# The first two activation tiles of a two-layer hybrid block, loaded and split one by one around the first weight tile

## Chip, cores, metric

The kernel runs on one core of a Trainium2 chip. The metric is the device time of one execution in microseconds (us). The engines are TensorE (PE, the matrix products), VectorE (DVE), ScalarE (ACT), GpSimd (POOL) and SyncE (SP), which issues the weight loads; data move through 16 DMA engines.

## What is computed

The reference runs two hybrid layers (retention, native sparse attention and a gated linear recurrence, side by side) and then two transformer layers (a dilated window mixer and a block attention mixer, each with a squared-ReLU MLP) on 256 tokens of width 1024. What matters here is its very first step, a matrix product of all tokens with the first input weight:

```python
def hybrid_layer(x, w_in, w_out, ln_g, ln_b, ...):
    proj = x @ w_in                 # x: 256 x 1024, w_in: 1024 x 3352
    ...                             # retention, sparse attention, recurrence
    y = jnp.concatenate([y_ret, y_nsa, y_lru], axis=-1) @ w_out
    return layer_norm(DEEPNORM_ALPHA * x + y, ln_g, ln_b)
```

## The kernel before

**Split products.** Every operand of the big products is held as two rounded parts: a high part, which ScalarE makes by copying the float32 value into a rounded type (`act_hi`, `w_hi`), and a low part, which VectorE makes as the value minus its high part (`act_lo`, `w_lo`). A product is three matmuls: high by high, high by low, low by high.

**Tiles.** The contraction of 1024 is cut into eight tiles k = 0 to 7 of 128 rows. An activation tile is 128 x 256 float32 (128 KB), a weight tile of the first three chunks 128 x 512 (256 KB). A chunk is four weight tiles. The first block of 512 output columns uses chunks 0 and 1. The first `HEAD` = 3 chunks (twelve weight tiles) are loaded, rounded and split tile by tile; all later chunks come whole, in one load of 1 MB (two smaller loads for the block named "window"), and are rounded whole by `split_hi` (L1396) and split whole by `split_lo` (L1881).

**Load order.** SP issues all weight loads from one queue. It begins with `x_pair(0)` (L590), activation tiles 0 and 1 in one load of 256 KB with 2 KB for each of 128 partitions, then weight tiles 0 and 1 (L598), then `x_pair(1)`, weight tiles 2 and 3, and so on. Chunk 3 is issued (L606) once `w_lo_done` says that chunk 0 is split; chunk 6 once chunk 3 is split.

**Rounding and splitting.** ScalarE and VectorE each walk the same list in order: `first_hi(0)` (L1503, both tiles of the pair in one instruction of 128 x 512), `head_hi(0)` (L1829), `head_hi(1)`, `first_hi(1)`, `head_hi(2)`, and so on; VectorE the same with `first_lo` (L2098) and `head_lo` (L2632). The raw activations lie in `y_tok`.

**TensorE at the start.** It waits for a small zeroed tile and multiplies it thirteen times with itself (`warm_up(13)`, L1366; each float32 product shows as two matmuls, 26 in all). Then `first_products` makes the six matmuls of k = 0 for both token halves (L861, L862, L865), the four that need only `w_hi` first. Then come k = 1 to 3, both halves of one k after the other, then k = 4 to 7 of one half after the other (L755 to L757), and `bias_vectors` (L871). ScalarE moves each finished half out of PSUM (L1414) in the middle of its list of rounding steps. GpSimd waits for the fourth `w_hi` before it issues three small constant loads, and for the rounding of chunk 3 before the next ones.

Of the kernel before, what the change touches and what calls it, by code (L numbers as in the profile page):

```python
# [21 lines left out]
S = 256  # L22
# [89 lines left out]
def build(nc, dram, out):  # L112
    F = mybir.dt.float32
    FR = mybir.dt.float32r
    I32 = mybir.dt.int32
    ALU = mybir.AluOpType
    ACT = mybir.ActivationFunctionType
# [47 lines left out]
    HEAD = 3  # L165
# [39 lines left out]
    X0, Y0, X1, Y1, DSW_U, DSW_Y, FFN0_U, MOBA_U, MOBA_Y, FFN1_U = range(10)  # L205
    LRU_CHUNK = [0, 1, 0, 1, 0, 0, 0, 0, 0, 0]
    ACT0 = [sum(ACTS[:i]) // 2 for i in range(11)]
# [29 lines left out]
    with ctx:  # L237
# [3 lines left out]
        def sem(name):  # L241
            return ctx.enter_context(nc.semaphore(name))
# [127 lines left out]
        ident_in = sem("ident_in")  # L370
        x_in = [sem(f"x_in{i}") for i in range(KD // 2)]
        x_rows = sem("x_rows")
        hot_in = sem("hot_in")
        gatew_zero = sem("gatew_zero")
        relb_in = sem("relb_in")
# [10 lines left out]
        at_hi = sem("at_hi")  # L386
# [171 lines left out]
        def first_acts(i):  # L558

            return y.rearrange("p t n -> p (t n)")[:, 512 * i:512 * i + 512]  # L560
# [26 lines left out]
        @block.sync  # L587
        def _(sp):
            def x_pair(i):
                sp.dma_start(first_acts(i), dram["x_features"][:, 2 * i:2 * i + 2, :].rearrange("p k n -> p (k n)")).then_inc(x_in[i], 16)  # L590

            x_pair(0)
            for c, (b, j) in enumerate(CHUNKS):
                d = BLOCKS[b]
                r0 = d["row0"] + 512 * j
                if c < HEAD:
                    for k in range(4):
                        sp.dma_start(w_raw[:, c, k, :], d["w"][r0 + 128 * k:r0 + 128 * k + 128, d["c0"]:d["c0"] + 512]).then_inc(first_in[4 * c + k], 16)  # L598
                        if k % 2 and 4 * c + k < KD - 1:
                            x_pair(2 * c + k // 2 + 1)  # L600
                    continue
                if c >= RAW:
                    sp.wait_ge(w_lo_done, split_count(c - RAW))
                for c0, at, n in pieces(b):
                    src = d["w"][r0:r0 + 512, c0:c0 + n].rearrange("(k p) n -> p k n", p=128)
                    sp.dma_start(w_raw[:, c % RAW, :, at:at + n], src).then_inc(w_arrived[c % RAW], 16)  # L606
            rows = out[0].rearrange("(t p) d -> p t d", p=128)
            for half in range(2):
                sp.wait_ge(acc_free[half], free_count(NB) - 1)
            sp.dma_start(rows[:, :, 0:512], x[:, :, 0:512]).then_inc(out_done, 16)  # L610
            for half in range(2):
                sp.wait_ge(acc_free[half], free_count(NB))
                sp.dma_start(rows[:, half, 512:1024], x[:, half, 512:1024]).then_inc(out_done, 16)
            sp.wait_ge(out_done, 16 * 3)
# [89 lines left out]
        def _(pe):  # L704
# [139 lines left out]
            def first_block():  # L844

                first_products()
                for k in range(1, 4):
                    for half in range(2):
                        tokens(0, half, (k,))
                for half in range(2):  # L850
                    tokens(0, half, range(4, 8))
                bias_vectors()

            def first_products():

                wh, wl = w_hi[:, 0, 0, 0:BLOCKS[0]["n"]], w_lo[:, 0, 0, 0:BLOCKS[0]["n"]]
                pe.wait_ge(at_lo, ACT0[X0] + 1)
                pe.wait_ge(w_hi_done, 1)
                for half in range(2):
                    o = sums(0, half)[:, 0:BLOCKS[0]["n"]]  # L860
                    pe.matmul(o, act_hi[:, 0, 128 * half:128 * half + 128], wh, start=True, stop=False)  # L861
                    pe.matmul(o, act_lo[:, 0, 128 * half:128 * half + 128], wh, start=False, stop=False)  # L862
                pe.wait_ge(w_lo_done, 1)
                for half in range(2):
                    pe.matmul(sums(0, half)[:, 0:BLOCKS[0]["n"]], act_hi[:, 0, 128 * half:128 * half + 128], wl, start=False, stop=False)  # L865
# [497 lines left out]
            def warm_up(count):  # L1363

                for _ in range(count):
                    pe.matmul(ps7[:, 0:128], still, still, start=True, stop=True)  # L1366

            still = st.rearrange("p a n -> p (a n)")
            pe.wait_ge(st_zero, 1)
            warm_up(13)  # L1370
            for l in range(LAYERS):
                hybrid(l)

# [11 lines left out]
        def _(act):  # L1385
# [442 lines left out]
                act.wait_ge(first_in[k], 16)  # L1828
                act.activation(w_hi[:, k // 4, k % 4, :], w_raw[:, k // 4, k % 4, :], ACT.Copy).then_inc(w_hi_done, 1)  # L1829

            for k in range(4 * HEAD):
                if k < KD and k % 2 == 0:
                    first_hi(k // 2)
                head_hi(k)
# [27 lines left out]
        def _(dve):  # L1862
# [766 lines left out]
            def head_lo(k):  # L2629

                dve.wait_ge(w_hi_done, k + 1)
                dve.tensor_tensor(w_lo[:, k // 4, k % 4, :], w_raw[:, k // 4, k % 4, :],  # L2632
                                  w_hi[:, k // 4, k % 4, :].bitcast(F), ALU.subtract).then_inc(w_lo_done, 1)

            for k in range(4 * HEAD):
                if k < KD and k % 2 == 0:
                    first_lo(k // 2)
                head_lo(k)
# [37 lines left out]
```

## Time and profile before

| what | us |
|---|---|
| median of 3 runs | 903.51 |
| lowest and highest of them | 903.37, 903.54 |
| the profiled execution's own time | 903.17 |
| its span, first to last instruction | 901.4 |
| TensorE busy in the span | 893.2 |

The span is what the trace shows; the profiled execution's own time is 1.77 us more, which lies around the span, and it was 0.34 us below the median of the runs. All times in the rows below are counted from the span's start.

### The profile page before, as it was taken

The numbers are of one execution on the slowest core, as the hardware profiler recorded it, in microseconds if no ns is written. First come the engines' busy times: TensorE is split into PE (matmuls) and PEld (weight loads), VectorE is DVE, ScalarE is ACT, GpSimd is POOL, SyncE is SP. The second block draws the span as 40 slices with busy tenths as digits, with TensorE's granted clock in tenths as the row PEclk, the third lists the DMA queues.
The fourth block names the chain that finished last, engine by engine and source line by source line (L and its number), as shares of the span: only waits on it lengthen the run. The fifth ranks groups of instructions, "written<-read, shape, count | busy, mean of one in ns | idle before, by whom it ended". The sixth has DMA issues, their size and how long they took to land.

```text
span 901.4 us, 13857 instructions
## 1 busy us (share of the span) xinstructions
PE 893.2 (99%) x5614; PEld 766.3 (85%) x5614; DVE 624.2 (69%) x1084; ACT 489.2 (54%) x733; POOL 40.2 (4%) x69
## 2 busy tenths in 40 slices
PE   9999999999999999999999999999999999999998
PEld 7887888987888888877999988888877799998886
DVE  5679978779978998785766644456788486664441
ACT  6555747555747755565555543346567465554330
POOL 2600010000000000000000000000000000000000
PEclk9999999999999999999999999999999999999999
DMA  8953454632445468641556565657463266655540
GB/s 293 316 202 95 139 187 145 211 118 94 141 141 170 157 239 250 190 116 47 189 188 187 188 192 181 220 160 231 135 210 119 92 203 219 188 187 189 185 162 24
DMA packets 79455, 155.55 MB, mean 173 GB/s; under 512 B 5656, under 2 KB 7864, under 8 KB 79392
## 3 DMA queue, kind: packets, MB, share of 16 engines
q1 hardware_dynamic: 75200, 142.81, 48.4%
q0 software_dynamic: 4192, 11.85, 4.8%
q8 instruction: 45, 0.74, 0.3%
q14 instruction: 18, 0.15, 0.0%
HBM read 153.54 MB, written 1.11 MB: 172 GB/s over the span
## 4 chain that ended last, share of the span: by engine, by line
PE 84%; DVE 8%; ACT 4%; DMA 2%; issue 1%; SPq 0%; DVEq 0%; ACTq 0%
PE ps L755 16%; PE ps L757 16%; PE ps L756 16%; PE ps L786 8%; PE ps L788 8%; PE ps L787 8%; DVE w_lo L1881 3%; DMA w_raw<-in_w_in 2%; ACT w_hi L1396 2%; PE ps_mid L965 1%; PE ps_mid L981 1%; PE ps L1056 1%; DVE area L2389 1%; PE ps_mid L755 1%; ACT y_tok L1522 1%
## 5 line engine op out<-in xcount | busy, mean ns | idle before, releaser
L1881 DVE TENSOR_TENSOR w_lo<-w_raw,w_hi 128x2048 fp32r<-128x2048 f32 x133 | 299.8, 2260 | 150.5 <-ACT w_hi L1396 150.3
L1396 ACT ACTIVATE w_hi<-w_raw 128x2048 fp32r<-128x2048 f32 x133 | 250.9, 1890 | 191.4 <-PE ps L757 141.6
L755 PE MATMUL ps<-w_hi,act_hi 128*128 128x512 f32 (+1 forms) x446 | 177.9, 399 | 0.5 <-ACT area L1414 0.2
L757 PE MATMUL ps<-w_hi,act_lo 128*128 128x512 f32 (+1 forms) x446 | 171.0, 384 | 0.0
L756 PE MATMUL ps<-w_lo,act_hi 128*128 128x512 f32 (+1 forms) x446 | 170.8, 383 | 0.0
L755 PE MATMUL ps<-w_hi,hid 128*128 128x512 f32 x296 | 116.2, 393 | 0.1
L757 PE MATMUL ps<-w_hi,hid 128*128 128x512 f32 x296 | 115.3, 389 | 0.0
L756 PE MATMUL ps<-w_lo,hid 128*128 128x512 f32 x296 | 115.2, 389 | 0.0
L786 PE MATMUL ps<-act_hi,w_hi 128*128 128x256 f32 x384 | 110.7, 288 | 0.0
L787 PE MATMUL ps<-act_lo,w_hi 128*128 128x256 f32 x384 | 107.5, 280 | 0.0
L788 PE MATMUL ps<-act_hi,w_lo 128*128 128x256 f32 x384 | 107.5, 280 | 0.0
L755 PEld LDWEIGHTS ps<-w_hi,act_hi 128*128 128x128 f32 x446 | 83.8, 188 | 18.9 <-issue 1.7
L757 PEld LDWEIGHTS ps<-w_hi,act_lo 128*128 128x128 f32 x446 | 83.7, 188 | 16.9
L756 PEld LDWEIGHTS ps<-w_lo,act_hi 128*128 128x128 f32 x446 | 84.0, 188 | 13.8
L786 PEld LDWEIGHTS ps<-act_hi,w_hi 128*128 128x128 f32 x384 | 72.3, 188 | 2.5 <-issue 1.1
L787 PEld LDWEIGHTS ps<-act_lo,w_hi 128*128 128x128 f32 x384 | 72.5, 189 | 0.0
L788 PEld LDWEIGHTS ps<-act_hi,w_lo 128*128 128x128 f32 x384 | 72.4, 189 | 0.0
L786 PE MATMUL ps<-early_acts,w_hi 128*128 128x256 f32 x256 | 71.8, 281 | 0.3 <-issue 0.3
L788 PE MATMUL ps<-early_acts,w_lo 128*128 128x256 f32 x256 | 71.5, 279 | 0.0
L787 PE MATMUL ps<-early_acts,w_hi 128*128 128x256 f32 x256 | 71.5, 279 | 0.0
L755 PEld LDWEIGHTS ps<-w_hi,hid 128*128 128x128 f32 x296 | 55.6, 188 | 12.6 <-DVE w_lo L1881 0.8
L757 PEld LDWEIGHTS ps<-w_hi,hid 128*128 128x128 f32 x296 | 55.6, 188 | 11.6
(369 smaller groups left out, 1239.5 us busy)
## 6 DMA issues: line engine op xcount, KB each, us to landing
w_raw<-in_ffn_w SPq DMA_DIRECT2D x64, 1024.0 KB, 5.4
w_raw<-in_w_in SPq DMA_DIRECT2D x21, 1024.0 KB, 5.7
w_raw<-in_a_w_qkv SPq DMA_DIRECT2D x18, 1024.0 KB, 5.0
w_raw<-in_b_w_qkv SPq DMA_DIRECT2D x12, 1024.0 KB, 5.1
w_raw<-in_w_out SPq DMA_DIRECT2D x8, 1024.0 KB, 5.0
w_raw<-in_b_w_o SPq DMA_DIRECT2D x4, 1024.0 KB, 5.0
w_raw<-in_w_in SPq DMA_DIRECT2D x12, 256.0 KB, 5.7
w_raw<-in_w_in SPq DMA_DIRECT2D x4, 512.0 KB, 3.6
```

The source lines that it names most:

```text
L755: pe.matmul(o, ah, wh, start=first, stop=False)
L756: pe.matmul(o, ah, wl, start=False, stop=False)
L757: mm = pe.matmul(o, al, wh, start=False, stop=last)
L786: pe.matmul(o, wh, ah, start=k == 0 and f % 2 == 0, stop=False)
L787: pe.matmul(o, wh, al, start=False, stop=False)
L788: mm = pe.matmul(o, wl, ah, start=False, stop=k == 7 and f % 2 == 1)
L965: mm = pe.transpose(ps4[:, 128 * i:128 * i + 128], nsa_weights(u)[:, at:at + 128], ident[:, :])
L981: pe.matmul(o[64 * e:64 * e + 64, :], v(0, e), nsa_PT[:, e, 0:S], start=p % 4 == 0, stop=False)
L1056: mm = pe.transpose(t_bank(2, u, g)[:, 128 * i:128 * i + 128], dil_weights(u)[:, at:at + 128], ident[:, :])
L1396: act.activation(w_hi[:, c % RING, :, 0:n], w_raw[:, c % RAW, :, 0:n], ACT.Copy).then_inc(w_hi_done, 1)
L1522: ins = act.activation(y[:, i % 2, 128 * k:128 * k + 128], act_bank[i][:, 128 * k:128 * k + 128], ACT.Identity, bias=gs[:, 1, kt:kt + 1], ...
L1881: dve.tensor_tensor(lo, w_raw[:, c % RAW, :, 0:n], hi.bitcast(F), ALU.subtract).then_inc(w_lo_done, 1)
```

## The change

Activation tiles 0 and 1 are loaded by a DMA each (`x_tile`), with 1 KB for each partition: tile 0 first, then weight tile 0, then tile 1, then weight tile 1. The later loads keep their order. ScalarE rounds tile 0 alone, then weight tile 0, then tile 1, then weight tile 1; VectorE subtracts in the same order. TensorE's first products wait for tile 0 alone (`x_tile_lo`), and the wait for the pair moves behind them, ahead of k = 1. The zero products are eleven and not thirteen.

```diff
-            x_pair(0)
+            def x_tile(k, arrived):
+                sp.dma_start(first_acts(0)[:, S * k:S * k + S], dram["x_features"][:, k, :]).then_inc(arrived, 16)
+
+            x_tile(0, x_tile_in)
...
                         sp.dma_start(w_raw[:, c, k, :], d["w"][r0 + 128 * k:r0 + 128 * k + 128, d["c0"]:d["c0"] + 512]).then_inc(first_in[4 * c + k], 16)
+                        if c == k == 0:
+                            x_tile(1, x_in[0])
...
                 first_products()
+                pe.wait_ge(at_lo, ACT0[X0] + 1)
                 for k in range(1, 4):
...
-                pe.wait_ge(at_lo, ACT0[X0] + 1)
+                pe.wait_ge(x_tile_lo, 1)
                 pe.wait_ge(w_hi_done, 1)
...
-            warm_up(13)
+            warm_up(11)
...
-            for k in range(4 * HEAD):
+            act.wait_ge(x_tile_in, 16)
+            act.activation(act_hi[:, 0, :], first_acts(0)[:, 0:S], ACT.Copy).then_inc(x_tile_hi, 1)
+            head_hi(0)
+            act.wait_ge(x_in[0], 16)
+            act.activation(act_hi[:, 1, :], first_acts(0)[:, S:2 * S], ACT.Copy).then_inc(at_hi, 1)
+            for k in range(1, 4 * HEAD):
                 if k < KD and k % 2 == 0:
                     first_hi(k // 2)
                 head_hi(k)
...
-            for k in range(4 * HEAD):
+            dve.wait_ge(x_tile_hi, 1)
+            dve.tensor_tensor(act_lo[:, 0, :], first_acts(0)[:, 0:S], act_hi[:, 0, :].bitcast(F), ALU.subtract).then_inc(x_tile_lo, 1)
+            head_lo(0)
+            dve.wait_ge(at_hi, ACT0[X0] + 1)
+            dve.tensor_tensor(act_lo[:, 1, :], first_acts(0)[:, S:2 * S], act_hi[:, 1, :].bitcast(F), ALU.subtract).then_inc(at_lo, 1)
+            for k in range(1, 4 * HEAD):
                 if k < KD and k % 2 == 0:
                     first_lo(k // 2)
                 head_lo(k)
```

## Rows read from the trace of the kernel before

**Rows 1.** The page's first two parts: busy time by engine, granted clock by slice.

```profile
PE 893.2 (99%) x5614; PEld 766.3 (85%) x5614; DVE 624.2 (69%) x1084; ACT 489.2 (54%) x733; POOL 40.2 (4%) x69
PEclk9999999999999999999999999999999999999999
```

**Rows 2.** Waits of TensorE, whole span: us in total, times, longest.

```profile
PE ps L861 <- ACT w_hi L1829: 0.6, 1, 0.6
...
PE ps L755 <- ACT area L1414: 0.2, 1, 0.2
```

**Rows 3.** Timeline, start of the kernel: start us, us, engine, instruction, [idle before].

```profile
1.05 4.96 PE L1366 MATMUL ps<-st 128*128 128x128 f32 x26 [1.05 <-DVE st L2627]
1.16 0.89 SPq L598 DMA_DIRECT2D w_raw<-in_w_in  x2
...
4.54 0.63 ACT L1503 ACTIVATE act_hi<-y_tok 128x512 fp32r<-128x512 f32 x1 [2.52 <-DMA y_tok<-in_x_features]
...
5.82 1.29 ACT L1829 ACTIVATE w_hi<-w_raw 128x512 fp32r<-128x512 f32 x2 [0.65 <-DMA w_raw<-in_w_in]
6.48 1.35 DVE L2632 TENSOR_TENSOR w_lo<-w_raw,w_hi 128x512 fp32r<-128x512 f32 x2 [0.59 <-ACT w_hi L1829]
...
6.59 0.47 PE L861 MATMUL ps<-w_hi,act_hi 128*128 128x512 f32 x1 [0.58 <-ACT w_hi L1829]
...
6.90 0.39 PE L862 MATMUL ps<-w_hi,act_lo 128*128 128x512 f32 x1
...
8.04 0.40 PE L755 MATMUL ps<-w_hi,act_hi 128*128 128x512 f32 x1
...
8.28 0.39 PE L756 MATMUL ps<-w_lo,act_hi 128*128 128x512 f32 x1
```

**Rows 4.** DMA issues at 0.74 (first pair) and 1.63 (weight tile 1): KB, us to landing.

```profile
y_tok<-in_x_features SPq DMA_DIRECT2D x1, 256.0 KB, 3.8
...
w_raw<-in_w_in SPq DMA_DIRECT2D x1, 256.0 KB, 4.8
```

**Rows 5.** Windows: length, busy of PE, PEld, DVE, ACT, POOL, PEclk, DMA share, GB/s.

```profile
3.00:3.50 0.50, 0.50 (x4) 0.50 (x4) 0.00 (x0) 0.00 (x0) 0.00 (x0) 1.00 0.43 107
5.00:12.00 7.00, 6.42 (x34) 5.31 (x33) 6.21 (x10) 6.22 (x11) 1.69 (x3) 1.00 1.05 393
```

**Rows 6.** DMA of 17.0:17.6, 1 KB packets of a later load among 2 KB ones.

```profile
DMA packets 211, 0.23 MB, mean 389 GB/s; under 512 B 6, under 2 KB 188, under 8 KB 211
```

**Rows 7.** Groups by line and form: instructions 256 elements wide (mean ns of one).

```profile
L1724 ACT ACTIVATE area<-area 128x256 f32<-128x256 f32 x2 | 0.8, 410 | 0.0
L2414 DVE TENSOR_TENSOR area<-area,st 128x256 f32<-128x256 f32 x2 | 0.8, 425 | 0.1
```

**Rows 8.** The chain of waits, window 15:32, in order of time.

```profile
9.79 8.65 DMA w_raw<-in_w_in
...
18.47 1.93 ACT w_hi L1396
...
20.42 2.31 DVE w_lo L1881
...
22.74 6.15 DMA w_raw<-in_w_in
...
30.73 0.58 ACT area L1414
```

**Rows 9.** Timeline of ScalarE ahead of chunk 3.

```profile
17.77 0.60 ACT L1414 ACTIVATE area<-ps 128x512 f32<-128x512 f32 x1 [0.73 <-PE ps L757]
```

**Rows 10.** Timeline of TensorE around 31 us.

```profile
30.83 0.29 PE L757 MATMUL ps<-w_hi,act_lo 128*128 128x280 f32 x1
31.36 0.40 PE L755 MATMUL ps<-w_hi,act_hi 128*128 128x280 f32 x1 [0.24 <-ACT area L1414]
```

**Rows 11.** Zero products in two windows: length, PE busy (x), PEld busy (x), PEclk, DMA share, GB/s.

```profile
1.00:4.60 3.60, 3.55 (x16) 3.55 (x17) 1.00 0.59 169
4.85:5.70 0.85, 0.85 (x9) 0.85 (x9) 1.00 1.05 393
```

More of the change, by code:

```diff
@@ L372, in build @@
         x_rows = sem("x_rows")
+        x_tile_in = sem("x_tile_in")
+        x_tile_hi = sem("x_tile_hi")
+        x_tile_lo = sem("x_tile_lo")
         hot_in = sem("hot_in")
```

## The prediction

> **What bounds the kernel now.** I read the page first. TensorE is busy 893.2 us of a span of 901.4 [rows 1], so the kernel is bound by its products, and only the 8.2 us in which TensorE stands still can be won by reordering. Its waits come next: 1.05 us at the very start [rows 3], 0.6 us ahead of the first real product, and 0.2 us for a bank that ScalarE clears [rows 2]. The change aims at the second. The timeline of the start [rows 3] shows what ends that wait. Activation pair 0 has landed at 4.54 (ScalarE starts on it then), ScalarE stands idle 0.65 us until weight tile 0 has landed, rounds it from 5.82 to 6.46, and TensorE's first product begins at 6.59. So the first product waits neither for activations nor for VectorE but for weight tile 0, whose load was issued at 1.16, just behind the pair. From 6.59 on TensorE doesn't pause. The last view is the chain of waits further on [rows 8 to 10], since a start that is earlier is worth something only if nothing downstream is held by another clock. There is such a place at 31.36.
>
> **The change, part by part.**
>
> *The load order.* Ahead of weight tile 0 there are 128 KB fewer. From 5 us on the DMA engines are full, at 393 GB/s [rows 5]; 128 KB at that rate are 0.33 us. Nothing in the start shows packets of 1 KB, but a load issued at 17.3 has them: 188 of 211 packets in that stretch are under 2 KB and the rate is still 389 GB/s [rows 6]. So I take the smaller packets as free and move the landing of weight tile 0 from about 5.79 to 5.46. The bounds: nothing, if the slow opening of the queue sets the landing (107 GB/s at 3.0 to 3.5 us [rows 5], so the engines weren't limited by bytes there), and 0.63 us, half of the 1.25 us between the two landings (4.54 and 5.79), if each byte ahead counts in full at that pace.
>
> *SP's queue.* The extra load takes one more issue slot, 0.47 us (two weight tiles took 0.89 us of issuing, with 0.05 between [rows 3]). Everything behind it is issued 0.47 us later: weight tile 1, the other three pairs, and ten more weight tiles; chunk 3 is not, since SP waits for a split there. Weight tile 1 was issued at 1.63 and landed 4.8 us later, at about 6.45, while the first pair, with nothing ahead of it, landed in 3.8 us [rows 4]. So some 1.0 us of its 4.8 are standing in line, more than 0.47, and the bytes ahead of it are as before: 128 + 256 + 128 KB. I take it to land at 6.45 again. The bound is 0.47 us later, at 6.92. Tile 1 needs 0.33 us behind weight tile 0 and lands near 5.8, before ScalarE asks for it.
>
> *ScalarE.* It rounds tile 0 in 0.41 us, the time of a 128 x 256 instruction [rows 7], somewhere from 4.2 to 4.5 on, well before weight tile 0. Then it rounds weight tile 0 from 5.48 to 6.12, tile 1 from 6.14 to 6.56, and weight tile 1 from 6.57. Before, weight tile 1 started at 6.46 or so (the pair of instructions from 5.82 takes 1.29 us [rows 3]). So the step that used to lie in ScalarE's idle time, half of the pair, now stands between the two weight tiles and costs 0.42 us, of which the earlier landing pays 0.33. All that is queued behind, pair 1 and the next weight tiles, goes 0.10 us later, until ScalarE has caught up with the loads (256 KB take 0.67 us at 393 GB/s, a rounding step 1.29 / 2 = 0.65). GpSimd's first constant loads, which wait for the fourth rounded weight tile, go 0.10 us later too; nobody needs them before 17 us.
>
> *VectorE.* Low part of weight tile 0: 6.14 to 6.83; of tile 1: 6.83 to 7.22 (0.42 us [rows 7]); of weight tile 1: from 7.22, when its high part is there, to 7.92. Before it was ready at 7.83 (6.48 + 1.35 [rows 3]). Late by 0.09 us.
>
> *TensorE.* The first product starts 0.33 us earlier, at 6.26. The six matmuls of k = 0 took from 6.59 to 8.04, 1.45 us [rows 3], and would be through at 7.71. But k = 1 needs the low part of weight tile 1 at 7.92. From the end of a high part to the product that waited for it were 0.13 us (6.46 to 6.59), so k = 1 starts at 8.05, where it stood before (8.04). A product after a pause holds back its follower by 0.31 us instead of 0.24 (6.59 to 6.90 against 8.04 to 8.28). Together k = 1 to 7 run 0.01 + 0.07 = 0.08 us later than before. In short: of the 0.33 us won ahead of k = 0 nothing is left at k = 1. k = 2 needs its operands some 0.3 us before it gets to them, so no more waits come.
>
> *The zero products.* Four fewer matmuls of 26 [rows 3], the last of nine that went at 0.85 us / 9 = 0.09 to 0.11 us each [rows 11], so TensorE is done with them at 5.56 and not at 6.01. The product it waits for comes at 6.26, so neither number is on the path; the pause ahead of it grows from 0.58 to 0.70 us. Free while the clock stays up; its price otherwise stands with the rivals.
>
> *What is left at the end.* At 31.36 TensorE has lost about 0.40 us: products of that width follow each other in 0.13 us, so the next one after 30.83 was due at 30.96 [rows 10]. It waits for ScalarE to clear a bank (L1414 at 30.73), which stands in ScalarE's list behind the rounding of chunk 6, which waits for its load, issued when chunk 3 was split at 22.72, which was rounded at 18.47, when its own load, issued at 9.79, had landed [rows 8]. That is a chain of loads, all the way back to the full DMA queue of the start; its bytes are the same after the change. So had TensorE come out of the start 0.3 us earlier, it would have waited 0.3 us longer at 31.36. A delay, on the other hand, of up to 0.40 us ends there too, as long as it doesn't touch the chain. It touches it in one place: ScalarE clears the second bank of block 0 from 17.77 to 18.37 just ahead of chunk 3 [rows 9], released by TensorE; 0.08 us later it ends at 18.45, and chunk 3 is rounded from 18.47 on, as before, or at most 0.05 us later. I take +0.05 us.
>
> One rule of the Trainium skill speaks against the change. "DMA: Bandwidth & Descriptors", section Bandwidth, asks for loads of 1 MiB or more, since smaller ones lose rate, and its fit (section Anatomy of one DMA) has 2 us fixed for each load plus the bytes at 436 GB/s. As an estimate from that page, two 128 KB loads done one after another would take 4.6 us where one of 256 KB takes 2.6, and the end would come 2.0 us later if nothing hid it. The trace disagrees for this queue: loads of 256 KB, issued 0.47 us apart, are in flight together and fill the engines [rows 4, 5], so a fixed part is paid side by side.
>
> **The sum.** 903.17 (the profiled execution's own time) + 0.05 = 903.2; the median of the runs was 0.34 above that execution, so 903.6.
>
> **The rivals.**
>
> *The start is passed on (faster).* If the landings of the whole queue move up with the smaller first load, chunk 3 lands earlier as well and 31.36 moves. For it: chunk 3's landing is at the head of the chain. Against it: its bytes and their rate are unchanged. It would give the 0.33 us of weight tile 0 at most: 903.2.
>
> *SP's extra slot comes through (a little slower).* If weight tile 1 lands 0.47 us later, its rounding starts at 6.94, k = 1 starts at about 8.4, and the banks of block 0 are cleared 0.4 us later, so chunk 3 is rounded at about 18.8; the whole chain and the end come 0.4 to 0.5 us later: 904.0. For it: the front of the queue was slow (107 GB/s), so latency rather than bytes may rule. Against it: the 1.0 us in line.
>
> *The clock falls (slower).* The zero products show two rates: 16 begun in 3.60 us, then 9 in 0.85 us [rows 11], that is 1.2 GHz and then 2.4 GHz, with the change near 4.8 us, 3.8 us after the first; the granted clock reads 1.00 in both windows and in all slices of the page [rows 1, 11]. If with the shorter run of zero products and the longer pause (0.70 us, 1.0 us if weight tile 0 lands no earlier) TensorE went back to 1.2 GHz until it had again worked 3.8 us, half of that is lost: +1.9 us, 905.4. It decides when one pause is enough to lower the clock. For it: the pause grows and its cover shrinks. Against it: the longest pause that this trace has behind the rise is 0.58 us and the rate stayed up. "TensorE: Matmul & The Clock Gate" of the Trainium skill (What's actually happening) says that the slow state is the default and activity releases it; so far the trace agrees.
>
> *The first product doesn't come earlier.* With the start-up ruling the landing, the first product stays near 6.59, tile 1 still stands in ScalarE's list, and k = 1 comes 0.4 us later; that is the price of the second rival, and is counted there.
>
> **How the numbers follow.** Forecast 0.60 (its own range 903.3 to 903.9), passed on 0.15, extra slot 0.20, clock 0.04; 0.01 is left for what I don't see, a shift of the later joints between the engines. The range leaves out the clock and that rest: 902.9 to 904.2, from the gain's upper bound of 0.63 us to the second rival with a little above it. No change, for this kernel, is within 0.2%, 1.8 us. Only the clock rival passes that bound, upward; so same 0.94, slower 0.05, faster 0.01.
>
> **What the profile after would show.** Right: the first product at 6.2 to 6.3; ScalarE with a 128 x 256 step between two weight tiles; a pause of TensorE of about 0.3 us ahead of k = 1, which starts at 8.0 to 8.1; chunk 3 rounded at 18.4 to 18.6; the product of 31.36 within 0.1 us of its old place. Wrong: k = 1 earlier than 7.8 (then VectorE wasn't what held it) or later than 8.3 (then SP's slot came through); 31.36 moved along with the start; products of k = 0 and 1 that follow in 0.43 us and not 0.23 (the clock).

## The result: a little slower, by the loads behind the first three

| | kernel before | changed kernel |
|---|---|---|
| median of 15 runs each | 903.07 | 904.27 |
| lowest and highest | 902.54, 904.55 | 903.54, 906.89 |
| the profiled execution's own time | 903.17 | 906.85 |
| its span | 901.4 | 904.3 |

The ratio is 1.0015 with an interval of 1.0008 to 1.0022, so some 0.7 to 2.0 us slower. The ratio itself is inside the 0.2% that the prediction called no change (its interval reaches just past it), and 904.27 is 0.07 us above the top of its range. The miss is larger than these 0.07 us: the kernel before came out at 903.07 here and not at the 903.51 that the forecast started from, so against the kernel before the prediction had allowed at most 0.7 us more and 1.2 were measured. The profiled execution of the changed kernel is one of its longest, and 2.55 us of its time lie outside the span, where the kernel before had 1.77. I therefore read from it where time goes, and take how much from the medians.

The page after, first its busy times (against [rows 1]), then the waits of TensorE (against [rows 2]):

```profile
PE 895.3 (99%) x5610; PEld 768.0 (85%) x5610; DVE 624.9 (69%) x1085; ACT 489.0 (54%) x734; POOL 40.2 (4%) x69
```

```profile
PE ps L763 <- DVE w_lo L2646: 1.4, 1, 1.4
```

TensorE's wait ahead of the first product is gone, as the change promised, and a longer one stands in its place: 1.4 us for a low part, where it was 0.6 us for a high part. The timeline of the start (against [rows 3]) says when:

```profile
1.05 5.06 PE L1375 MATMUL ps<-st 128*128 128x128 f32 x22 [1.05 <-DVE st L2641]
4.55 0.63 ACT L1838 ACTIVATE w_hi<-w_raw 128x512 fp32r<-128x512 f32 x1 [0.92 <-DMA w_raw<-in_w_in]
5.09 0.40 ACT L1844 ACTIVATE act_hi<-y_tok 128x256 fp32r<-128x256 f32 x1
5.77 0.77 PE L870 MATMUL ps<-w_hi,act_hi 128*128 128x512 f32 x1
5.91 0.63 ACT L1838 ACTIVATE w_hi<-w_raw 128x512 fp32r<-128x512 f32 x1 [0.42 <-DMA w_raw<-in_w_in]
7.63 0.40 PE L763 MATMUL ps<-w_hi,act_hi 128*128 128x512 f32 x1
8.56 0.63 ACT L1512 ACTIVATE act_hi<-y_tok 128x512 fp32r<-128x512 f32 x1 [2.02 <-DMA y_tok<-in_x_features]
10.59 0.50 PE L763 MATMUL ps<-w_hi,act_hi 128*128 128x512 f32 x1 [1.43 <-DVE w_lo L2646]
```

Weight tile 0 is there at 4.55, 1.2 us sooner than in the profile of before; the first product begins at 5.77, 0.82 us sooner; k = 1 at 7.63, 0.41 us sooner. Then ScalarE stands idle for 2.02 us, until activation pair 1 has landed at 8.56, and TensorE for 1.43 us ahead of k = 2, at 10.59. Before, k = 2 followed k = 1 without a pause, six products of 0.23 us behind 8.04, at 9.41. So 0.41 us of lead at k = 1 is 1.18 us of delay at k = 2. (The profile of before is late in this place: in the four other profiles with its loads, shown below, weight tile 0 landed at 5.1 to 5.2 and not at 5.79, and weight tile 1 at 5.8 to 5.9 and not at 6.45. Against them the changed kernel has weight tile 0 only 0.6 to 0.7 us sooner, and weight tile 1 not sooner at all.) The DMA issues (KB, us to landing) of weight tile 0, weight tile 1 and pair 1, against [rows 4]:

```profile
w_raw<-in_w_in SPq DMA_DIRECT2D x1, 256.0 KB, 3.4
...
w_raw<-in_w_in SPq DMA_DIRECT2D x1, 256.0 KB, 3.8
...
y_tok<-in_x_features SPq DMA_DIRECT2D x1, 256.0 KB, 6.0
```

Both weight tiles took less time to land than in that profile, weight tile 1 3.8 us instead of 4.8. Pair 1, issued at 2.57, took 6.0 us. In the kernel before it was issued at 2.10 and took 5.0. What the DMA engines moved meanwhile, in the window 5 to 8 us (length, busy of PE, PEld, DVE, ACT, POOL, PEclk, DMA share, GB/s), first of the kernel before:

```profile
5.00:8.00 3.00, 2.42 (x16) 1.98 (x15) 2.21 (x4) 2.30 (x5) 0.00 (x0) 1.00 1.04 375
```

and of the changed kernel:

```profile
5.00:8.00 3.00, 3.00 (x14) 2.65 (x13) 1.72 (x3) 1.12 (x3) 0.00 (x0) 1.00 0.89 262
```

262 GB/s instead of 375 over 3 us is 0.34 MB less, as much as 0.86 us of the full rate of 393 GB/s [rows 5]. Up to 5 us the changed kernel had moved only 0.05 MB more (163 GB/s against 153), so most of this is a hole and not a head start: by 9.5 us it is 0.32 MB behind (229 GB/s from the start against 263). The stream as a whole fell behind just when weight tile 0 had come early.

How that delay reaches the end, by the chain of waits in order of time (start, length), against [rows 8, 10]:

```profile
18.81 0.24 PE ps L765
19.07 0.30 ACT area L1423
...
19.57 1.92 ACT w_hi L1405
21.51 2.30 DVE w_lo L1895
23.83 6.26 DMA w_raw<-in_w_in
30.11 0.84 ACT w_hi L1405
...
31.93 0.58 ACT area L1423
32.56 0.39 PE ps L763
```

ScalarE clears the second bank of block 0 at 19.07 and not at 17.77 [rows 9], so chunk 3 is rounded at 19.57 and not at 18.47; split, reload and the rounding of chunk 6 follow in unchanged steps, and the product that stood at 31.36 stands at 32.56: 1.2 us later, the difference of the medians. The product ahead of it began at 32.13 and it was due 0.13 us later, at 32.26, so TensorE still loses 0.30 us there, where it lost 0.40. That 1.2 and 1.2 agree to the tenth is in part chance: in three other profiles with the loads of before this product stands at 30.90 to 31.09.

This profile's span is 2.9 us longer, though, not 1.2. The rest lies in two stretches of products 256 columns wide, in windows of 60 us (length, PE busy with its count, PEclk, DMA share, GB/s), first of the kernel before and then of the changed one:

```profile
450.00:510.00 60.00, 60.00 (x517) 1.00 0.61 193
745.00:805.00 60.00, 60.00 (x516) 1.00 0.61 196
```

```profile
450.00:510.00 60.00, 60.00 (x512) 1.00 0.59 186
745.00:805.00 60.00, 60.00 (x511) 1.00 0.64 202
```

About five products fewer fit into 60 us. From the start of one to the start of the next (the counts of a window take in those under way at its edge) the trace has 117.8 ns instead of 116.7, although TensorE is busy throughout and the granted clock is the same. Against the kernel before, TensorE's products stand 1.2 us later ahead of the first such stretch, 2.03 behind it and 2.88 behind the second, so each costs some 0.85 us. Whether this belongs to the change is asked below.

### The profile page after: what moved, and what is told of

Its sections match the earlier page's. It is cut to its first block, busy times and chain, and to the rows that moved or that the text cites. A ratio compares the mean times of both kernels' runs of the same rounds, so it can differ in the third digit from the quotient of the medians.

```text
span 904.3 us, 13853 instructions
## 1 busy us (share of the span) xinstructions
PE 895.3 (99%) x5610; PEld 768.0 (85%) x5610; DVE 624.9 (69%) x1085; ACT 489.0 (54%) x734; POOL 40.2 (4%) x69
## 4 chain that ended last, share of the span: by engine, by line
PE 85%; DVE 7%; ACT 4%; issue 1%; DMA 1%; SPq 0%; DVEq 0%; ACTq 0%
PE ps L763 17%; PE ps L765 16%; PE ps L764 16%; PE ps L794 8%; PE ps L795 8%; PE ps L796 8%; DVE w_lo L1895 3%; ACT w_hi L1405 2%; PE ps_mid L974 1%; PE ps_mid L990 1%; PE ps L1065 1%; DMA w_raw<-in_w_in 1%; DVE area L2403 1%; DMA y_tok<-in_x_features 1%; PE ps_mid L763 1%
## 5 line engine op out<-in xcount | busy, mean ns | idle before, releaser
L765 PEld LDWEIGHTS ps<-w_hi,hid 128*128 128x128 f32 x296 | 55.6, 188 | 11.6
```

The lines of the kernel that those rows point to most:

```text
L765: mm = pe.matmul(o, al, wh, start=False, stop=last)
```

## The experiments

Two questions. Which part of the change costs the time: the zero products, the rounding tile by tile, or the loads? And what is it about the loads: their number, their order, or the way the activations lie in memory? The runs of one group below were made on one chip and share one median of before. "Joint" is the start of the product that stood at 31.36 in the profile of before; "pair 1" is when the second activation pair had landed.

### First group: both kernels again, and the zero products

The median of before was 902.99. The first two have no edit: the changed kernel, and the kernel before under another name.

> The changed kernel as it is, a second time. Queue theory (an extra load in front makes activation pair 1 land late, at 8.5 us, in every execution): the profile again has ScalarE start on pair 1 at 8 us or later, TensorE again waits 1 us or more ahead of k = 2, and the time is 1.0 to 1.4 us above before. Clock theory (fewer zero products cost it): pair 1 lands near 7.1, no long wait ahead of k = 2, yet the time is still 1.0 us or more above before. Spacing theory (the two up projections of the MLPs run their products 118 ns apart instead of 117 from time to time, 0.86 us for each): the 256 column products of up0 and up1 are 1% apart between executions of the same kernel, and this explains 0, 0.9 or 1.7 us of any difference between two profiles.

**e1** measured 903.87, ratio 1.0010 (1.0001 to 1.0019). The joint is at 32.29, k = 2 at 10.51 behind k = 1 at 7.47, pair 1 at 8.4. Its window:

```profile
5.00:8.00 3.00, 2.94 (x14) 2.28 (x13) 1.72 (x3) 1.10 (x3) 0.00 (x0) 1.00 0.87 268
```

> The kernel before, a second time. Queue theory: pair 1 lands near 7.1 as before, TensorE reaches k = 2 near 9.4; time equal within 0.3 us. If landings of the first 10 us are chance, pair 1 lands anywhere from 7 to 8.6 here too. Spacing theory: up0 and up1 may show 117.8 ns between products in place of 116.7 in this execution.

**e2** measured 902.80, ratio 0.9998 (0.9989 to 1.0007). The first product came at 5.99 without a wait, k = 2 at 8.83, pair 1 at 6.6, the joint at 31.00; 391 GB/s in 5 to 8 us.

```profile
5.21 1.27 ACT L1829 ACTIVATE w_hi<-w_raw 128x512 fp32r<-128x512 f32 x2
5.99 0.47 PE L861 MATMUL ps<-w_hi,act_hi 128*128 128x512 f32 x1
```

So the start of one and the same kernel moves by 0.6 us between executions, and the joint by 0.36, but the joint and pair 1 come nowhere near the changed kernel's. The first product does: the wait for weight tile 0 that the change was made to remove isn't in this execution at all. The tile landed at 5.19 and not at 5.79, its high part was ready at about 5.8, and the zero products filled the time until then.

```diff
-            warm_up(13)
+            warm_up(11)
```

> The kernel before with eleven zero products, nothing else. Queue theory: 0 to 0.2 us above before. Clock theory: 0.8 us or more above before, nearly all of what the change costs, with the first products at half rate or the clock's rise later. Spacing theory: no change of the median beyond 0.2 us unless the count of TensorE instructions sets the spacing, in which case both up projections show 117.8 ns and the time is 1.7 us above.

**e3** (this line alone, in the kernel before) measured 903.14, ratio 0.9999 (0.9991 to 1.0008); joint 30.90, pair 1 at 7.1. **e4** is the other corner, the changed kernel with `warm_up(13)` again:

```diff
-            warm_up(11)
+            warm_up(13)
```

> The changed kernel with thirteen zero products. Queue theory: as the changed kernel, 1.0 to 1.4 us above before. Clock theory: within 0.3 us of before. Spacing theory by instruction count: both up projections back at 116.7 ns, within 0.3 us of before.

It measured 903.94, ratio 1.0009 (1.0000 to 1.0018), with pair 1 at 8.3, k = 2 at 10.38, 271 GB/s and the joint at 32.70. The number of zero products is worth nothing that these medians show: the four corners are 902.80, 903.14, 903.94 and 903.87. The slow first product of the profile after (0.77 us, at the lower of the two rates) isn't the cause: in e1 it takes 0.48 us, at the higher, and the delay is there.

Eleven zero products do leave one mark, outside the span. In every kernel with thirteen or twenty (before included) the time of an execution is 1.74 to 1.95 us more than its span (258 executions in the five groups). In the eight sets of runs with eleven it is 2.07 to 3.10 us more in 26 of 88 executions, e3 among them, whose only edit this is (3 of 11, against none of 33 of before beside it). It is too rare to move most medians, and no row shows what the time is spent on.

### Second group: loads or rounding, and the order

The median of before was 903.30. e5 takes the load order of the change and nothing else: the pair is rounded and split whole, with thirteen zero products.

```diff
-            x_pair(0)
+            x_tile(0, x_tile_in)
...
+                        if c == k == 0:
+                            x_tile(1, x_in[0])
...
+                if i == 0:
+                    act.wait_ge(x_tile_in, 16)
```

> Only the load order of the change: tile 0, weight tile 0, tile 1, weight tile 1, then as before; rounding, splitting and products in pairs as before, thirteen zero products. Loads theory (the split load itself leaves a hole in the stream behind weight tile 1): activation pair 1 is complete only at 8.3 to 8.5 us and the time is 0.9 us above before. Rounding theory (the order on ScalarE and VectorE delays the later tiles): pair 1 complete at 6.6 to 7.1, time within 0.3 us of before.

**e5** measured 904.46, ratio 1.0015 (1.0006 to 1.0024); pair 1 at 8.1, joint 32.35. The window and TensorE's wait:

```profile
5.00:8.00 3.00, 2.50 (x12) 2.16 (x11) 1.27 (x3) 2.73 (x4) 0.00 (x0) 1.00 0.86 270
```

```profile
PE ps L867 <- DVE act_lo L2106: 0.5, 1, 0.5
```

Pair 1 and the joint:

```profile
8.15 0.63 ACT L1511 ACTIVATE act_hi<-y_tok 128x512 fp32r<-128x512 f32 x1 [0.42 <-DMA y_tok<-in_x_features]
32.35 0.40 PE L761 MATMUL ps<-w_hi,act_hi 128*128 128x280 f32 x1 [0.24 <-ACT area L1420]
```

It has the whole loss, with none of the rounding and none of the zero products. One more thing is to be seen: TensorE doesn't wait 1.4 us ahead of k = 2 here, since it began 0.9 us later, at 7.47, behind a wait for the whole pair; yet the joint is as late. What counts is when pair 1 has landed, not where TensorE spends the pause.

e6 is the opposite: rounding, splitting and waits of the change with eleven zero products, and the pair in one load.

```diff
             x_pair(0)
...
+            act.wait_ge(x_in[0], 16)
+            act.activation(act_hi[:, 0, :], first_acts(0)[:, 0:S], ACT.Copy).then_inc(x_tile_hi, 1)
+            head_hi(0)
...
+            act.activation(act_hi[:, 1, :], first_acts(0)[:, S:2 * S], ACT.Copy).then_inc(at_hi, 1)
```

> Only the compute side of the change: the pair is loaded in one as before, but rounded and split tile by tile around weight tile 0, eleven zero products. Loads theory: pair 1 complete at 6.6 to 7.1, time within 0.3 us of before, k = 1 up to 0.1 us late. Rounding theory: 0.9 us above before.

**e6** measured 903.55, ratio 1.0003 (0.9994 to 1.0013); joint 31.09, pair 1 at 6.7:

```profile
5.00:8.00 3.00, 3.00 (x13) 2.37 (x12) 2.46 (x5) 2.71 (x6) 0.00 (x0) 1.00 1.06 373
```

```profile
6.74 0.63 ACT L1510 ACTIVATE act_hi<-y_tok 128x512 fp32r<-128x512 f32 x1
31.09 0.40 PE L761 MATMUL ps<-w_hi,act_hi 128*128 128x280 f32 x1 [0.17 <-ACT area L1421]
```

The loss is in the loads. e7 keeps two loads, but issues both ahead of weight tile 0 (cut here: ScalarE waits for both tiles, as in e5); e8 keeps one load of the pair, but puts weight tile 0 ahead of it.

```diff
-            x_pair(0)
+            x_tile(0, x_tile_in)
+            x_tile(1, x_in[0])
```

> The kernel before with its first pair as two loads of 128 KB, both ahead of weight tile 0; compute as before. If one more load or packets of 1 KB make the hole: pair 1 complete at 8.3 us or later, 0.9 us above before. If it is the order (a weight tile in second place, the opening of the queue shared by both tensors): within 0.3 us of before.

**e7** measured 903.68, ratio 1.0003 (0.9993 to 1.0013), joint 31.87. Pair 1 was there at 7.3, but pair 2 only at 10.0; 325 GB/s. A half-way result in the trace; the median doesn't tell it from before.

```diff
-            x_pair(0)
...
+                        if c == k == 0:
+                            x_pair(0)
```

> The kernel before with weight tile 0 loaded ahead of the first pair, the pair in one load; compute as before. If one more load or packets of 1 KB make the hole: no hole, pair 1 complete near 7 us, within 0.3 us of before. If it is the order: pair 1 complete at 8 us or later, 0.9 us above before.

**e8** measured 904.78, ratio 1.0017 (1.0007 to 1.0026), joint 32.21, pair 1 at 8.1, k = 2 at 10.23:

```profile
5.00:8.00 3.00, 2.92 (x16) 2.46 (x14) 1.81 (x3) 1.78 (x3) 0.00 (x0) 1.00 1.00 328
```

No load more than before and no byte, and the loss is complete. So an extra load isn't needed for it; an early weight tile is enough. (Its profile has the wide spacing in both stretches, so its 1.5 us need not all come from the start: the joint is 0.9 to 1.3 us later than in the profiles with the loads of before.) Weight tile 0 landed at 3.5 and the pair at 5.25, and both were paid for by what came behind.

### Third group: the layout of the activations, and two other orders

The median of before was 903.35. The activations lie in memory as 128 rows of 8 KB, of which a pair's load takes 2 KB each. e9 is the changed kernel with them laid out pair by pair, so that the rows of one load are 2 KB apart:

```diff
-    a["x_features"] = a["x"].reshape(S, KD, 128).transpose(2, 1, 0)
+    a["x_features"] = a["x"].reshape(S, KD // 2, 2, 128).transpose(1, 3, 2, 0).reshape(KD // 2, 128, 2 * S)
```

> The changed kernel with the input copy of the activations laid out pair by pair, so that the rows of a load lie 2 KB apart in memory and not 8 KB; loads, sizes and order as in the change. Address theory (activation rows far apart, read while weight rows are read, make the slow packets at 5 to 7 us): pair 1 complete at 7 us or earlier, the 0.9 us are gone. Order theory (a weight load in the opening of the queue is enough, wherever the rows lie): pair 1 complete at 8 us or later, 0.9 us above before.

**e9** measured 903.86, ratio 1.0009 (0.9999 to 1.0018), with its ten runs in two groups (902.8 to 904.0 and 904.6 to 905.5). The upper group is that of the time outside the span, 2.5 to 2.8 us in all four of its executions; half of the ten have it. By the spans alone the median is 0.2 us above before (901.8 and 901.6). Its profile is of the first group: joint 31.40, pair 1 at 7.3, pair 3 at 11.35:

```profile
5.00:8.00 3.00, 2.84 (x12) 2.14 (x10) 1.55 (x4) 1.45 (x4) 0.00 (x0) 1.00 0.88 268
```

Inconclusive: the rate is as low as in the changed kernel, yet pair 1 is early. e10 is the changed kernel with both tiles ahead of weight tile 0:

```diff
             x_tile(0, x_tile_in)
+            x_tile(1, x_in[0])
...
-                        if c == k == 0:
-                            x_tile(1, x_in[0])
```

> The changed kernel with one swap: both activation tiles ahead of weight tile 0, each still a load of its own; compute as in the change, eleven zero products. Order theory: pair 1 complete before 7.5 us, within 0.5 us of before. If the compute side and the extra load together are needed for the loss: 0.9 us above before.

**e10** measured 904.12, ratio 1.0010 (1.0000 to 1.0019), joint 32.44, 326 GB/s; pair 1 came at 6.65 but pair 2 at 10.3 and pair 3 at 12.2. The first pair of the stream was in time and a later one wasn't. It repeats e7's loads and shows, as e7 does, that the hole in the stream can open further back.

```diff
-            warm_up(13)
+            warm_up(20)
```

> The kernel before with twenty zero products, which hold the first real product back to 7.2 us or so, 0.6 us later; loads as before. Price of a late start: up to 0.4 us are swallowed by the wait at 31 us, so 0.2 to 0.3 us above before. Delay theory of the spacing (118 ns follows from a late TensorE start): up0 or up1 shows 117.8 ns. Loads theory of the spacing: both at 116.7 ns.

**e11** delays TensorE alone and leaves the loads as they are. It measured 905.32, ratio 1.0022 (1.0012 to 1.0032). Two products of its timeline, and a wait that the kernel before hasn't:

```profile
7.84 0.48 PE L861 MATMUL ps<-w_hi,act_hi 128*128 128x512 f32 x1
...
32.24 0.29 PE L755 MATMUL ps<-w_hi,act_hi 128*128 128x280 f32 x1
```

```profile
PE ps L786 <- ACT gate_c L1418: 0.5, 1, 0.5
```

The first product is 1.25 us later than in the profile of before and the joint 0.88, with no pause ahead of it any more: about 0.4 us were swallowed on the way, as the prediction had it (against e2 it is 1.85 and 1.24, so 0.6). But the end is 2.1 us later (spans of 903.5 and 901.4). Another 0.76 us are lost near 176 us, where TensorE waits for a gate, and two times 0.22 later. A delay at the start isn't only carried along, it can grow. e12 issues both first pairs ahead of weight tile 0:

```diff
             x_pair(0)
+            x_pair(1)
...
-                        if k % 2 and 4 * c + k < KD - 1:
+                        if k % 2 and 0 < 4 * c + k - 1 < KD - 2:
```

> The kernel before with activation pairs 0 and 1 both ahead of weight tile 0. Order theory: no slow stretch at 5 to 7 us; weight tile 0 complete about 0.65 us later than in before, the first product as much later, and the time at most 0.3 us above before. If any departure from the old order brings the slow stretch: the third to fifth load 1.2 us late, 0.9 us above before.

**e12** measured 903.87, ratio 1.0006 (0.9996 to 1.0015). Weight tile 0 landed at 6.7, so the first product came at 7.46, 0.87 us late; the joint is at 31.87, 0.50 late: 0.37 us swallowed. 363 GB/s. Activations first is the mirror of the change: it loses at the start and nearly keeps the stream (pair 3 at 11.2, against 10.6 to 11.0).

### Fourth group: layout and order crossed

The median of before was 902.98. e13 is the kernel before with e9's layout, e15 is e8 with it, e16 is e9's kernel once more; e14 splits weight tile 0 instead of the pair.

> The kernel before with only the input copy of the activations laid out pair by pair (rows 2 KB apart). Address theory: the first pair lands earlier and the stream has no slow stretch, activation pair 3 complete at 10.6 us or earlier; time 0 to 0.5 us below before, as the rest is bound by later loads. Order or load count theory: as before, pair 3 complete at 10.6 to 11.0.

**e13** measured 902.70, ratio 0.9996 (0.9987 to 1.0005), joint 30.12. The window, and the issue of the first pair, against 3.8 us [rows 4]:

```profile
5.00:8.00 3.00, 3.00 (x18) 2.46 (x17) 2.29 (x4) 2.50 (x4) 0.00 (x0) 1.00 1.04 382
```

```profile
y_tok<-in_x_features SPq DMA_DIRECT2D x1, 256.0 KB, 2.7
```

The first load is there 1.1 us sooner when its rows are 2 KB apart; the later ones gain less (pair 1 at 6.1 here, at 6.65 and 6.8 in e17 and e18, hardly sooner than the 6.6 to 7.1 of the loads of before), and the median hardly anything.

```diff
+                        for q in range(2 if 4 * c + k == 0 else 1):
+                            n0, n1 = (256 * q, 256 * q + 256) if 4 * c + k == 0 else (0, 512)
-                        sp.dma_start(w_raw[:, c, k, :], ...)
+                            sp.dma_start(w_raw[:, c, k, n0:n1], ...)
```

> The kernel before with weight tile 0 loaded in two halves of 256 columns (packets of 1 KB), so one load more in the queue but activations first and whole. Load count theory: pair 3 complete at 11.8 to 12.4 us, 0.5 to 1.1 us above before. Address or order theory: pair 3 complete at 11.2 or earlier, within 0.3 us of before.

**e14** measured 903.70, ratio 1.0005 (0.9996 to 1.0014), joint 32.39, 308 GB/s, pair 3 at 11.6. TensorE waits 0.9 us at the joint, more than in any other run here, and chunk 3 itself has to be waited for (0.15 us ahead of its rounding). Another load more near the head of the queue, another stream that falls behind, with the activations whole.

> Weight tile 0 ahead of the first pair as in e8, but with compact activations. Address theory: pair 3 complete at 11.2 or earlier (12.0 with spread rows), and most of the 1.5 us of e8 gone. Order theory: as e8, pair 3 complete near 12.0, 1.2 to 1.7 us above before.

**e15** measured 903.27, ratio 1.0000 (0.9990 to 1.0010), joint 31.45, pair 3 at 10.7, 353 GB/s against 328 in e8. That is level with the kernel before, but the layout helps that kernel too. The fair partner is e13, the order of before with the same rows: against it e15 has 0.6 us more in the median (902.70) and 1.3 us at the joint (30.12). So the order still seems to cost something with compact rows, perhaps less than the 1.5 us of e8; medians of ten runs, each known to some 0.9 us, can't settle it.

> The changed kernel with compact activations, a second time. Address theory: TensorE near its old place at 31 us again, 0 to 0.5 us above before; if e9's good profile was chance: pair 3 complete near 12.3 and 0.9 us above before.

**e16** measured 903.98, ratio 1.0008 (0.9999 to 1.0018), joint 31.87, k = 2 at 9.98, pair 1 at 7.9, 283 GB/s. Together with e9 the changed load order with compact rows stays slow in the stream; the layout brings the joint forward (31.40 and 31.87 against 32.29 to 32.70). It does the same for the order of before (30.12 to 30.79 against 30.90 to 31.36), and against e13 the changed order costs e16 1.3 us in the median and 1.75 at the joint: what the order costs is still there.

### Fifth group: is the compact layout a gain?

The median of before was 903.64. e17 is e13's kernel, e18 is it with eleven zero products.

> The old order with compact activation rows, again, in five rounds. If the gain is real: 0.3 to 0.8 us below before, TensorE 0.5 to 1.2 us earlier at 31 us. If e13 was chance: within 0.2 us of before. Spacing: 116.7 ns in both up projections if the wide spacing belongs to the changed loads.

**e17** measured 902.95, ratio 0.9996 (0.9988 to 1.0005), joint 30.79, first pair landed 2.6 us after its issue.

> The same with eleven zero products. In e13 the first product began at 5.49 us, the moment that the zero products ended, so eleven could let it start up to 0.2 us earlier; the wait at 31 us swallows it: the same time as e17 within 0.3 us. If the first product then runs before the clock has risen, nothing is won either.

**e18** measured 903.40, ratio 1.0004 (0.9994 to 1.0013), joint 30.75, and one of its two stretches has the wide spacing, although its loads are those of before. The compact layout with the old order gave 0.9996 twice, both times with 1 inside the interval: no slower, not shown to be faster.

### What they say together

| loads | GB/s in 5 to 8 us | pair 1 at | joint | medians over before, us |
|---|---|---|---|---|
| of before (profile shown, e2, e3, e6, e11) | 358 to 391 | 6.6 to 7.1 | 30.90 to 31.36; e11 32.24 | -0.2, +0.15, +0.25; e11 +2.0 |
| of the change (profile after, e1, e4, e5) | 262 to 271 | 8.1 to 8.6 | 32.29 to 32.70 | +1.2, +0.9, +0.95, +1.2 |
| one load more, elsewhere (e7, e10, e14) | 308 to 326 | 7.3, 6.65, 6.5 | 31.87 to 32.44 | +0.4, +0.8, +0.7 |
| weight tile 0 first (e8) | 328 | 8.1 | 32.21 | +1.5 |
| both first pairs first (e12) | 363 | 6.0 | 31.87 | +0.5 |
| of before, compact rows (e13, e17, e18) | 344 to 382 | 6.1, 6.65, 6.8 | 30.12 to 30.79 | -0.3, -0.7, -0.2 |
| of the change, compact rows (e9, e16) | 268, 283 | 7.3, 7.9 | 31.40, 31.87 | +0.5, +1.0 |
| weight tile 0 first, compact rows (e15) | 353 | 6.4 | 31.45 | +0.3 |

The five times of the loads of before leave no overlap with the four of the change in rate, landing and (e11 aside, where TensorE itself is delayed) joint. That these loads land late and move the joint rests on this; that they cost about 1 us rests on four medians 0.9 to 1.2 us over their partner, against three within 0.25 us of theirs. The wide spacing of the late products is a thing by itself: it is in 9 of 40 stretches of the 20 profiles, among them kernels with the loads of the change (the profile after, e5) and without (e8, e12, e15, e18), not in e1 and e4, and never in the unchanged kernel (two profiles) or e3, e6 and e11. It makes an execution that has it once 0.85 us longer, or 1.7 with both. Whether the change makes it more frequent is open.

## Why the prediction was wrong, step by step

**The bound and the start.** Right in kind for the execution that was read: the wait for weight tile 0 was the one to be removed, and it is gone. But it was taken from a single profile. In the other four with the loads of before the tile landed at 5.08 to 5.24, earlier than the 5.46 forecast for the change, and in e2 the first product came at 5.99 with no pause ahead of it, so there was less to win than one profile showed. The sizes were off on the good side. The prediction had weight tile 0 at 5.46, with 5.16 as the earliest; it came at 4.55. It had the first product at 6.26 and the zero products off the path ("Free while the clock stays up"); it came at 5.77, because the 22 zero products ended only just before (all at the lower of the two rates, 5.06 us in the timeline), and they, not the weight tile, now hold it. k = 1 was to stand where it stood, at 8.05; it came at 7.63. (VectorE's sum is 0.03 us short, since 6.83 and 0.42 are 7.25 and not 7.22; nothing hangs on it.)

**The step that failed** is "SP's queue", with the sentence that closed TensorE's part: "k = 2 needs its operands some 0.3 us before it gets to them, so no more waits come." Both asked of a load only how many bytes lie ahead of it. For weight tile 1 they are as before, and I let it stand for "everything behind it": the forecast held no later landing for any load behind weight tile 1. For pair 1 they are as before as well, yet it landed 1.46 us later: 0.47 us of later issue, as the step knew, and 1.0 us more from issue to landing, which by the rule of bytes should have shrunk by 0.47. 1.46 less the 0.3 us of slack are the 1.2 us of k = 2. (Over all nine profiles with these loads, four after the change and five before, pair 1 is 1 to 2 us late.) That the cause lies in the load order is shown (e5 has it all; e6 and e3 have the other parts of the change and nothing of it; e4 has it without the fewer zero products). That the stream's rate falls with it is shown. Why it falls isn't.

**The mechanism downstream** was right, and only fed with the wrong number. The step "what is left at the end" named the one place at which a delay touches the chain, the bank cleared just ahead of chunk 3, and the 0.40 us that can end at 31.36. It put 0.08 us in, and got 0.05 out. 1.3 us go in, and 1.2 come out, in the profile after; e1, e4 and e5 give 0.9, 1.3 and 1.0. A delayed start gives what the step says: e11, where TensorE alone is late, loses 0.37 on the way to the joint, e12 0.37. The 0.40 us of pause ahead of the joint are no constant, though: e2 has 0.5 us there and e3 none.

**The rivals.** "SP's extra slot comes through" had the place (a load behind the extra one is late, TensorE waits for it, block 0's bank is late) and 904.0, the nearest of the times. But it was weight tile 1 that was to be late, by the slot of 0.47 us and no more. It landed at 5.89 to 6.31 in the four profiles of the changed loads, against 6.45 in the profile of before and 5.80 to 5.88 in the four others: early or up to 0.5 us late, as one chooses the partner, and k = 1 stands at 7.47 to 7.90 in the changed kernel with and without its fewer zero products, against 7.36 to 8.04 in the kernel before and e3. What was late by more than any of this, and in every profile, was the load after it. "The start is passed on" fell: the start did move up, by more than its 0.33 us, and the end went the other way. "The clock falls" fell as written, since no pause brought the lower rate back, not even the 1.43 us ahead of k = 2; e3 and e4 show no cost of fewer zero products. The first two products of k = 0 did run slowly in the profile after, behind zero products that were slow throughout, and e6's first one too, with the loads of before; in e1 they did not, and the loss was there as well.

**The rule of small loads.** The Trainium skill ("DMA: Bandwidth & Descriptors", section Bandwidth) was set aside because loads in flight together had filled the engines. Both the section's rates and the fixed 2 us were measured on loads that GpSimd issues, and these are issued by SyncE, which the prediction didn't say. Its direction was right for this case: one more small load near the head of the queue gave 262 to 326 GB/s where 358 to 391 were had. Its sum (2.0 us for the two halves one after the other) has no counterpart, for the first half was there sooner than the pair had been and the second only 0.2 to 0.4 us later (3.2 and 4.7 to 4.9 us, against 4.5), and e8 loses as much with the same loads in another order, of which that section says nothing.

**What stays open**: why the stream falls behind when a weight tile's load stands early or one more load is put in. Whether rows of the activations 8 KB apart have a part in it isn't shown: with rows 2 KB apart everything comes sooner, but against e13 the order of e8 still has 0.6 us more (e15, where the 8 KB rows had 1.5), and the changed order 1.3 (e16, where they had 0.9 to 1.2) and its low rate. Which resource it is, no row names. A weight tile's rows are apart by the width of its matrix, and were not laid out otherwise.

## What to carry to other kernels

When a load is moved ahead, check the landing of the next several loads, not only of those that the first work waits for: here weight tile 0 came 0.6 to 1.3 us sooner, the second activation pair 1 us later at least, and only that one counted. Find the place where two chains meet (here a bank cleared just ahead of a chunk's rounding) and compute how much delay reaches it, since a start that is won is swallowed there and a start that is lost is not. For a difference of 0.1% test the parts alone, as with loads without rounding and rounding without loads, and take several profiles of the same kernel before the change is planned, because its own start moves by 0.6 us: here the wait to be removed was in one profile of the kernel before and not in the other.

## What the runs showed of the chip that was not expected

- The order and number of the first loads changed the rate of the whole stream: 262 to 271 GB/s against 358 to 391 from 5 to 8 us, with the same bytes in all.
- With the loads of before, the first load of 256 KB lands 2.6 to 2.7 us after its issue with rows 2 KB apart (e13, e17, e18), and 3.7 to 3.8 us with rows 8 KB apart (five profiles).
- The moment at which the zero products change from the lower to the higher rate moves from run to run while their start doesn't (1.05 us in nearly all): near 4.0 us in e7, 4.8 in the kernel before, near 5.9 in e11, and only after the last of 22 in the profile after, e6 and e9; in e5, e12, e14 and e15 even the last of 26, begun at 6.55, still went at the lower rate.
- Products of 256 columns have two spacings, 116.7 and 117.8 ns from start to start, each steady over a whole stretch at the same granted clock, worth about 0.85 us per stretch.
- A delay of TensorE of 1.25 us at the start cost 2.1 us of span (e11), although 0.4 us of it were swallowed by the first joint.
- The time of an execution outside its span is 1.74 to 1.95 us in 258 executions of kernels with thirteen or twenty zero products, and 2.07 to 3.10 us in 26 of 88 with eleven.
